# Dense attention with keys on the partitions: scores computed transposed, the maximum subtracted inside the product

## The reference

```python
# mla: q, k of 96 numbers a head, v of 64; 1024 queries, 1024 keys
s = jnp.einsum('bqhd,bkhd->bhqk', q_blk, k).astype(jnp.float32) * scale
p = jax.nn.softmax(s, axis=-1).astype(v.dtype)
return jnp.einsum('bhqk,bkhd->bqhd', p, v)
# diff_attend: q, k of 32 numbers a map; 1024 queries (and 256 context queries in layer 0), 1280 keys
s = jnp.einsum('bqhmd,bkhmd->bhmqk', q, k).astype(jnp.float32) * (q.shape[-1] ** -0.5)
# gqa_attend: q, k of 64 numbers a head; the same queries and keys
s = jnp.einsum('bqhgd,bkhd->bhgqk', qg, k).astype(jnp.float32) * (d ** -0.5)
```

## Time and profile before

| | us |
|---|---|
| median of 3 runs (lowest, highest) | 4858.2 (4856.95, 4863.97) |
| the profiled execution | 4862.26 |
| its span in the profile | 4860.6 |
| PE busy | 3743.6 (77%) |
| DVE busy | 2448.4 (50%) |
| ACT busy | 2216.2 (46%) |
| POOL (GpSimd) busy | 913.2 (19%) |

### The profile page before, as it was taken

The page is one execution under the profiler, slowest core; times in us unless marked ns, Lnnn a source line. Parts: engine busy times, 40 slices in busy tenths (PEclk is TensorE's granted clock), DMA queues, the critical chain, the costliest instruction groups (busy, mean ns, idle before and its releaser), DMA issues. The chain is left out here.

```text
span 4860.6 us, 70948 instructions
## 1 busy us (share of the span) xinstructions
PE 3743.6 (77%) x24823; PEld 3029.3 (62%) x24823; DVE 2448.4 (50%) x4502; ACT 2216.2 (46%) x3911; POOL 913.2 (19%) x749
## 2 busy tenths in 40 slices
PE   3986786877459999278988869675778997879557
PEld 3974565656348888266766657554656775658446
DVE  2114453442477888475425545455575425546454
ACT  1215454651047777322226657554432226657442
POOL 0213000000026665043540000000034440000002
PEclk7998898988679999689999989887889998989878
DMA  6227413303879999322323242422232223232423
GB/s 218 100 108 224 97 37 77 106 31 131 274 270 391 398 393 345 115 88 83 103 80 70 77 87 57 87 84 76 80 101 67 98 93 76 78 77 58 104 81 94
DMA packets 328087, 634.15 MB, mean 130 GB/s; under 512 B 115048, under 2 KB 171272, under 8 KB 326696
## 3 DMA queue, kind: packets, MB, share of 16 engines
q1 hardware_dynamic: 292436, 510.46, 33.4%
q0 software_dynamic: 33840, 113.66, 7.3%
q10 hardware_dynamic: 1444, 5.30, 0.3%
HBM read 490.39 MB, written 138.95 MB: 129 GB/s over the span
## 5 line engine op out<-in xcount | busy, mean ns | idle before, releaser
L1882 PE MATMUL pr_ps<-pr_wH,hT_part 128*128 128x512 f32 x1120 | 445.6, 398 | 0.0
L1652 ACT ACTIVATE ex_high<-ex_ring 128x2048 fp32r<-128x2048 f32 x192 | 368.6, 1920 | 98.0 <-PE ex_pg L1628 39.6
L1698 DVE TENSOR_TENSOR ex_ring_part<-ex_ring,ex_high 128x2048 fp32r<-128x2048 f32 x144 | 372.4, 2586 | 51.3 <-ACTq L1653 39.6
L1882 PE MATMUL pr_ps<-pr_wH,x_sb_part 128*128 128x512 f32 x896 | 363.9, 406 | 22.5 <-DVEq L1955 22.5
L1882 PE MATMUL pr_ps<-pr_w_part,x_sb_part 128*128 128x512 f32 x896 | 356.6, 398 | 0.0
L1144 DVE TENSOR_REDUCE aa_nm<-aa_ps 128x1 f32<-128x1280 f32 (+1 forms) x144 | 197.7, 1373 | 305.7 <-PE aa_ps L1045 304.9
L1593 POOL TENSOR_TENSOR ex_ring_part<-ex_ring,ex_high 128x2048 fp32r<-128x2048 f32 x48 | 239.3, 4985 | 216.5 <-ACTq L1653 216.5
L1055 PE MATMUL aa_ps<-ident,aa_prob 128*128 128x128 f32 x1312 | 209.0, 292 | 61.8 <-ACTq L1181 60.1
L1177 ACT ACTIVATE aa_prob<-aa_ps,aa_nm 128x512 f32<-128x512 f32 (+2 forms) x272 | 211.1, 776 | 87.9 <-DVEq L1145 44.4
L1144 DVE TENSOR_REDUCE ab_nm<-ab_ps 128x1 f32<-128x1280 f32 (+1 forms) x108 | 148.3, 1373 | 194.7 <-PE ab_ps L1045 194.4
L1882 PEld LDWEIGHTS pr_ps<-pr_wH,hT_part 128*128 128x128 f32 x1120 | 216.5, 193 | 47.1
(11 more groups left out here) (356 smaller groups left out, 9203.6 us busy)
## 6 DMA issues: line engine op xcount, KB each, us to landing
ex_ring<-in_w_gate SPq DMA_DIRECT2D x64, 1024.0 KB, 9.6
ex_ring<-in_w_up SPq DMA_DIRECT2D x64, 1024.0 KB, 8.2
ex_ring<-in_w_down SPq DMA_DIRECT2D x64, 1024.0 KB, 7.9
z_d<-pr_zT POOLq DMA_DIRECT2D x120, 256.0 KB, 3.0
rt_mw<-in_w_ada SPq DMA_DIRECT2D x14, 2048.0 KB, 16.0
pr_w<-in_w_in SPq DMA_DIRECT2D x14, 2048.0 KB, 9.0
mod_w<-in_w_ada SPq DMA_DIRECT2D x10, 2048.0 KB, 13.2
proj<-pr_raw POOLq DMA_DIRECT2D x60, 256.0 KB, 2.3
```

Source lines behind the costliest of these rows:

```text
L1652: scalar.activation(wH[:, c % HL].bitcast(F32R), w_sb[:, c % SL], ACT.Copy)
L1698: vector.tensor_tensor(w_part[:, c % SL].bitcast(F32R), w_sb[:, c % SL], wH[:, c % HL], ALU.subtract)
L1882: mm = tensor.matmul(ps[:, g % 4, :], x.bitcast(F32R), w[:, c % 2, kk, :].bitcast(F32R), start=kk == 0 and i == 0, stop=kk == KC - 1 and i ...
```

## The change

A new stage, `stage_turned`, takes the place of `stage_attention` for am, aa0, aa1, ab0 and ab1. It works in blocks of 512 queries (256 context queries in layer 0) of a pair of heads. A step `g` is one tile of 128 keys against a block's queries for both heads:

- `search` (PE and DVE): q as the stationary operand against up to 512 keys, in one pass of `qA` and `kA`, into one of two banks `mp`; DVE reduces each piece to a maximum. There are 24 pieces for a block of 1280 keys, 16 for 1024. The pieces of block B+1 are worked off four to a step during block B; those of block 0 come ahead of everything.
- `row`: PE transposes the negated maxima, ACT copies them, SP writes them to DRAM and reads them back into one more partition of q (`shift_row`), against a row of ones in k; so the score product subtracts the maximum. The first scores of a block wait for that DMA (`rw`).
- `scores`: k is the stationary operand, queries are the moving one; the result has keys on the partitions. ACT takes Exp of 1024 columns (two heads, two banks) into `pT`, a ring of six. `values` takes `pT` as it is, two steps at a time at odd steps.
- The sum of the probabilities: DVE adds steps 0 and 1 and the last one, GpSimd steps 2 to the last but one, DVE adds the two accumulators; a product with ones (`sums`) adds over the partitions; DVE takes the reciprocal of 512 columns and multiplies; PE transposes the output (`turned`), ACT copies it, GpSimd stores it.

`stage_attention`, still used for ad and ac, now always puts `scores` ahead of `transposes` and the maximum ahead of `turned_part`. The bias and mask of ac are loaded as its `extra` instead of under ab. x and the context are reloaded from ACT's queue at step 4 of aa.

```diff
@@ stage_attention
-                        if h < n and LAG == 1:
+                        if h < n:
                             scores(h)
                         if 0 <= g < n:
                             transposes(g)
-                        if h < n and LAG == 2:
-                            scores(h)
...
-                    dve.wait_ge(extra_ready, 16)
+                    dve.wait_ge(extra_ready, 16 * n_extra)
...
-                        if LAG == 2:
-                            turned_part(g)
...
-                        if LAG == 1:
-                            turned_part(g)
+                        turned_part(g)
@@ stage_turned
+    def stage_turned(name, dq, pairs, nq, sk, blocks, aside=None):
+        dv, RP = 64, 6
...
+            pcs = [(b, m) for b in ahead if b < NBLK for m in range(len(maxima(b)))]
+            return pcs[4 * i:4 * i + 4]
+
+        def row_at(B):
+            if B == 0:
+                return -1
+            return 2 + max(g for g in range(TOT) if any(b == B for b, _ in searched(g)))
+        rows_at = [row_at(B) for B in range(NBLK)]
+        D_AT, F_AT, S_AT = 4, 6, 8
...
+        def on_dve(blk, i):
+            return size[blk] <= 2 or i in (0, 1, size[blk] - 1)
...
+            def passes(b, j, q, kk):
+                if dq == 32:
+                    return [(kA[0:97, b, j, kk], qA[0:97, b, j, q])]
+                if dq == 64:
+                    return [(kA[:, b, j, kk], qA[:, b, j, q]), (kB[0:65, b, j, kk], qB[0:65, b, j, q])]
+                return [(kA[0:97, b, j, kk], qA[0:97, b, j, q]), (kA[0:96, b, j, kk], qB[0:96, b, j, q]),
+                        (kB[0:96, b, j, kk], qA[0:96, b, j, q])]
...
+            @block.sync
...
+                def row(B):
+                    p, blk = divmod(B, NB)
+                    q0, qn, _, _ = blocks[blk]
+                    sp.wait_ge(sr, slot_row(B) + 1)
+                    n = 2 * qn // P
+                    sp.dma_start(nm_d[B:B + 1, 0:n * P].rearrange("o (c q) -> (o c) q", q=P), nmT[0:n, :]).then_inc(nw, 16)
+                    sp.wait_ge(nw, 16 * (B + 1))
+                    if B:
+                        sp.wait_ge(rw, 16 * B)
+                    sp.dma_start(shift_q[shift_row:shift_row + 1, p % 2, :, q0:q0 + qn],
+                                 nm_d[B:B + 1, 0:n * P].rearrange("o (j q) -> o j q", j=2)).then_inc(rw, 16)
...
+            @block.tensor
...
+                for g in range(TOT + F_AT):
+                    if g < TOT:
+                        scores(g)
+                        for x, (B, m) in enumerate(searched(g)):
+                            search(B, m, pieces_before[g] + x)
+                    if g % 2:
+                        for B in range(NBLK):
+                            if end(B) + D_AT == g:
+                                sums(B)
+                        for x in (g - 3, g - 2):
+                            if 0 <= x < TOT:
+                                values(x)
+                    if g in out_at:
+                        turned(out_at[g])
+                    for B in range(1, NBLK):
+                        if rows_at[B] == g:
+                            row(B)
...
+            @block.vector
...
+                for g in range(TOT + F_AT):
+                    if g < TOT:
+                        for x, (B, m) in enumerate(searched(g)):
+                            search(B, m, pieces_before[g] + x)
+                    if 0 <= g - 2 < TOT:
+                        add(g - 2)
+                    for B in range(NBLK):
+                        if end(B) + D_AT == g:
+                            normalised(B)
@@ first_block, second_layer
-        stage_attention("am", 2, 2, mla, QD, S, every)
+        stage_turned("am", QD, [mla(p // 2, p % 2) for p in range(H1 // 2)], S, S, [(0, 512, 0, S), (512, 512, 0, S)])
...
-        dense = [[(0, S2)]] * ST + context
+        dense = [(0, 512, 0, S2), (512, 512, 0, S2)] + ([] if last else [(S, CTX, S, S2)])
...
-        stage_attention(f"aa{l}", 2, 2, maps, DK, S2, dense, aside=streams)
+        stage_turned(f"aa{l}", DK, [maps(p // 2, p % 2) for p in range(MAPS // 2)], rows, S2, dense, aside=streams)
...
+        stage_turned(f"ab{l}", HD, [grouped(0, p) for p in range(HB // 2)], rows, S2, dense)
...
-            stage_attention(f"ab{l}", 1, 3, grouped, HD, S2, dense, aside=biases)
...
-            stage_attention(f"ac{l}", 1, 3, near, HD, S2, tiles, bias, prepare=masked, apart=True,
+            stage_attention(f"ac{l}", 1, 3, near, HD, S2, tiles, bias, extra=biases, n_extra=2, prepare=masked, apart=True,
```

More of the change, by code:

```diff
@@ L884, in stage_attention @@
     def stage_attention(name, loops, pp, addr, dq, sk, tiles, add_bias=None, extra=None,
-                        aside=None, prepare=None, apart=False):
+                        aside=None, prepare=None, apart=False, n_extra=1):
         nq, nt_k, dv = len(tiles), sk // P, 64
@@ L2226, in biases @@
                 sp.dma_start(G[:, :, 0:NEARK], a["nat_rpb_2"][l]).then_inc(s, 16)
-                return 2
             def masked(dve):
```

292 lines of the change are left out of this document (added).

## The result

The changed kernel took 5035.8 us (median of four runs, 5035.3 to 5051.0) against 4860.2 for the kernel before, run beside it: a ratio of 1.0369 (95% interval 1.0347 to 1.039). The forecast was 5017, range 4930 to 5145. The profiled execution has a span of 5033.9 us, granted clock 0.851 on the mean.

What follows compares the result with a forecast made beforehand. DVE's work plus an idle chain through the row's DRAM trip was taken to bound turned blocks. Five turned stages +165, biases +12, reordering -18 gave +159: 5021, less 4, 5017 us; range 4930 to 5145.

Steps and rivals of the forecast that it cites:

- Its mechanism: Turned blocks: DVE's work, then a chain with DVE idle until the next scores; aa 36.6 us a block against 32.8.
- the end of the chain: Block's end: the next block's first score waits for the row's way over DRAM, 5.0 us; PE's remaining work is done.
- rival 2: DVE additions against GpSimd in turned blocks: exclusion costs 2.5 instead of 0.5 us a block, +72, 5089 us; chance 0.10.
- done by then: Block's tail: PE's remaining work, 2.6 us, is finished before the row of maxima is back from DRAM.
- The context blocks of layer 0: Small blocks of 256 context queries in layer 0's aa and ab: about 4 us each, mostly in the gap.
- The reordering: stage_attention in ad and ac: ac -15 (bounds -30 and +5), ad -3, together -18 us.
- The biases: Bias and mask loads moved from under ab to ahead of ac's own loads: +6 twice, +12 us (bounds 0 and 18).
- Rival 1: TensorE dearer in turned blocks: the heads' 512-column products don't overlap, or the clock falls; +122, 5139 us; chance 0.20.
- Rival 3: Turned blocks: the wait at a block's end goes, leaving DVE's work alone; -301, 4716 us; chance 0.12.
- DVE is then never free: Steps 0 to 5 of an aa or ab block: search and other DVE work fill them; aa 26.0 us.
- turning point: Hidden tail: the change's sign turns where 4.4 of the 9.75 us at a block's end are hidden (159/36).

Runs made afterwards that it cites:

- kernel with the short reciprocal: Changed kernel with the reciprocal in aa and ab covering 16 columns instead of 512, leaving most queries unnormalised: 4963.0 us, ratio 1.0218.
- one with slower transfers: Changed kernel with the row of maxima copied within SBUF by eight small transfers instead of a pair over DRAM: 5154.0 us, ratio 1.0596.
- its own kernel: Changed kernel with TensorE's turn of the row of maxima one step after the last search piece instead of two: 5049.8 us, ratio 1.039.
- the kernel with the order alone: Kernel before with only stage_attention reordered, scores ahead of transposes and maximum ahead of DVE's copy; also called the reordered kernel: 4810.4 us, ratio 0.9902.
- the mixed one with three pieces: Three search pieces a step and the row one step behind, with the earlier step's products moved between an odd step's second and third piece: 5033.6 us, ratio 1.0355.
- one step's products a step: Three search pieces a step, with one step's products between the second and third piece at every step instead of two steps' at odd ones: 4994.4 us, ratio 1.0267.
- the spread kernel: Changed kernel with three search pieces a step instead of four, and the row of maxima one step behind the search instead of two: 5072.1 us, ratio 1.0437.
- the mixed one with four pieces: Changed kernel, still four search pieces a step, with the earlier step's products between an odd step's second and third piece: 5052.9 us, ratio 1.04.

## Why the prediction was right, and where it was off

Its mechanism stands for aa and ab: DVE's work and then an idle tail of about 10 us make a block, and that is more than eight steps of the old form. The kernel with the short reciprocal showed that DVE's work is on the path, the one with slower transfers that the row is. For am the end of the chain was wrong: there TensorE's own work comes last, not the row. That the total came so close is partly luck. The five turned stages cost 208.5 us where 165 was forecast, ad and ac gave 32.8 where 6 was, and the two errors largely cancel.

- DVE: a search phase of 26.4 to 26.6 us where 26.0 was forecast. The terms, of the kernel after by form:

```profile
L1519 DVE TENSOR_REDUCE aa_part<-aa_mp 128x1 f32<-128x512 f32 x256 | 177.0, 691 | 173.9 <-PE aa_mp L1396 153.6
L1519 DVE TENSOR_REDUCE aa_part<-aa_mp 128x1 f32<-128x256 f32 x144 | 61.1, 424 | 33.2 <-PE aa_mp L1396 18.2
L1546 DVE RECIPROCAL aa_rB<-aa_mp 128x512 f32<-128x512 f32 x16 | 53.7, 3357 | 7.3 <-PE aa_mp L1437 6.1
L1535 DVE TENSOR_TENSOR ab_accd<-ab_accd,ab_pT 128x1024 f32<-128x1024 f32 x12 | 22.3, 1860 | 55.9 <-ACTq L1488 55.2
L1540 DVE TENSOR_TENSOR aa_accd<-aa_accd,aa_accp 128x1024 f32<-128x1024 f32 x16 | 19.6, 1226 | 19.6 <-POOL aa_accp L1587 18.4
```

  Reductions 691 and 424 ns (692 and 425 forecast), the reciprocal 3357 (3.35 us). By the repeat count of 8 in the Trainium skill (VectorE: DVE Perf Modes, "First, the fixed hardware budget") it would be an estimated 4.3 us; the measurement decides for 3.36.
- The exclusion of DVE and GpSimd: the addition to the running sum in ab took 1860 ns on the mean instead of 1226, in aa 1376. With am (1498 ns, eight times) that is 150 x 16 + 634 x 12 + 272 x 8 ns = 12 us, 0.3 for each of 43 blocks where 0.5 was taken: rival 2 is out. Nearly all of it is in 13 additions (2 in am, 5 in aa, 6 in ab), of 1.4 to 3.3 us. Each began while a GpSimd addition was running and ended 1.07 to 1.09 us after that one's end. The rule of the Trainium skill (SBUF — State Buffer, "SBUF: two separate sides") fits: the whole GpSimd instruction is waited out. The price is small because so few of DVE's additions met one.
- The tail in aa: 9.75 forecast from DVE's end to the next scores, 9.89 measured (4271.42 to 4281.31), but two terms were wrong and cancelled, which is luck. TensorE needed 6.05 us to the row's transpose instead of 3.9, since its first eight products fell into the stretch at 1.2 GHz (3.28 us against 1.94) and the two steps' scores wait for ScalarE. The row took 3.2 us over DRAM instead of 5.0: the small transfers in the earlier trace rows were the nearest rows, and too dear. The prediction also called TensorE's remaining work "done by then" with time to spare; it ended 0.6 us before the row in aa, and after it in am. An earlier row had at most that to win in aa, and its own kernel showed that it delays the work behind it.
- The pitches, as means from a stage's first block to its last, taken between their first scores: aa 37.9 (37.1 forecast), ab 38.0 (38.0), both of the last layer, am 33.0 (31.1). First scores 37.7 us after the first load in am (37), 37.5 and 46.0 in the last layer's aa and ab (39.5, 49). The last layer came out at +49.3 and +53.3 (forecast +44 and +56).
- The sum was 16 us under the measured change of the stretches (159 against 175.7). The mis-sized terms are these. am, 304.2 against 288: its seven pitches (36.0 the first, then 31.7 to 33.4) had a mean of 33.0 us instead of 31.1, which makes 13 of the 16. The context blocks of layer 0, forecast at 4 us each "mostly in the gap": the three blocks of a pair in aa took 82.8 us, 7.8 more than two of 37.5; seven times the missing 3.8 is 27, and aa and ab of layer 0 came out 13.4 and 10.8 above the forecast. The reordering was forecast at -18 and brought -44.4 (9.2 in ad, 18.6 and 16.6 in ac by the kernel with the order alone); the bound for ac was -30. The biases were forecast at 12; ac paid 11.6 by the comparison with the reordered kernel, and 6.6 were left net of what ab pays when it has them.
- Rival 1, the dearer TensorE. Its first half is refuted: the two heads' products of 512 columns do overlap, eight in 1.94 us with 0.60 for the last, 0.45 for a pair where I had 0.43. Its second, the lower clock, came true (aa 0.75, 0.92 before). What it cost was not measured by itself, but ab of the last layer has blocks of both kinds. Where the eight products around DVE's end ran at 0.50 (3.68 us, twice), the next scores came 11.2 and 11.5 us after DVE's end and the pitch between first scores was 40.5 and 40.4; where they ran at 1.00 (1.94 us, three times), 8.5 to 8.9 us and, but for the first block, 37.6. By their own extra time the slow products at the start of the tails, 13 in aa, 3 in ab and 3 in am, come to an estimated 29 us, a quarter of the 122.
- Rival 3, a hidden tail, was tried in five orders. Tails of 7.1, 9.1, 6.7, 12.1 and 5.6 us came with search phases of 32.6, 31.9, 30.9, 26.7 and 32.0. "DVE is then never free" holds for the changed kernel's order only: the tail is where TensorE's and ScalarE's other work is done. TensorE was busy 28.0 to 35.0 us of each of these blocks, DVE 22.3 to 23.1. In the four orders that shortened the tail, the work moved out of it made the search phase 4.3 to 6.0 us longer. That the two PSUM buffers of the search between two engines that work in order are the reason was not tested. The prediction's turning point for this rival was also too low: it divided 159 us by 36 blocks, but only 31 have a successor in their stage, which makes 5.1 us.

What stays open: three orders (the changed kernel's, the mixed one with three pieces, one step's products a step) gave a pitch near 37.5 us in aa with quite different tails; the spread kernel and the mixed one with four pieces gave 40 to 41. Whether something but chance ties the block to such values was not tried. Nor was a third PSUM buffer for the search.

## What to carry to other kernels

When two in-order engines hand tiles to each other through two buffers, a stall at the end of a block is not a reserve: look at what the other engines do in it before moving work out of it, and look in each stage, since another engine can come last there. A reordering that touches two queues has to be made in both; one half alone can cost more than the whole brings. And take a bundle of edits apart: here a few lines of reordering were worth 1.0% and stood inside a change that lost 3.7%.

## What the runs showed of the hardware that was not expected

- A RECIPROCAL of 512 float32 columns takes 3357 ns, 6.6 a column, and TensorE, which could have gone on, waited 3.47 us behind it through the PSUM buffers.
- Eight transfers of 512 bytes within SBUF from one queue took 4.93 us to issue and 6.1 us to the first product that read them; one pair over DRAM took 3.2 us altogether.
- A VectorE addition with both inputs in SBUF that began beside a GpSimd addition ended 1.07 to 1.09 us after the end of that one, up to 3266 ns where it takes 1226 alone.
- In am additional matmuls raised TensorE's granted clock from 0.86 to 0.92 and left the stage at 304.2 us: what the clock gave, if anything, the additional work took.
